# Gate projection with its two halves of the weights side by side

## The reference

```
px = (rmsnorm(x, norm1_g[l]) * (1.0 + sc1) + sh1) @ w_in[l] + b_in[l]
g = p[..., GATE_OFF:SGU_OFF]          # 16 columns
gates = (g[0], log_sigmoid(g[1]), g[2], log_sigmoid(g[3]))
b = cumsum(log_forget)                # per chunk of 128 tokens
```

## Time and profile before

| what | value |
|---|---|
| median of 3 runs | 2589.0 us |
| the profiled execution's own time | 2588.8 us |
| its span, first to last instruction | 2586.0 us |
| TensorE busy | 2521.5 us (98%) |
| VectorE busy | 1395.6 us (54%) |
| ScalarE busy | 777.0 us (30%) |
| GpSimd busy | 1548.5 us (60%) |
| granted TensorE clock, mean | 0.997 |

### The profile page before, as it was taken

One profiled execution on the slowest core, in us unless ns is written; L12 is line 12 of the kernel. 1 busy time (PEld: TensorE's weight loads), 2 busy tenths in 40 slices (PEclk: granted clock), 3 DMA queues, 4 the chain that ended last, 5 costly groups with the idle time before them and its releaser, 6 DMA issues.

```text
span 2586.0 us, 39643 instructions
## 1 busy us (share of the span) xinstructions
PE 2521.5 (98%) x14594; PEld 2083.6 (81%) x14594; DVE 1395.6 (54%) x2065; ACT 777.0 (30%) x1620; POOL 1548.5 (60%) x1625
## 2 busy tenths in 40 slices
PE   6999999999999999999999999999999999999999
PEld 5888988888888886888788887778888887777876
DVE  5864556742853758726433333444544555557854
ACT  3224353111111123245321212222222222443544
POOL 2433244765766665543777777776666676546563
PEclk9999999999999999999999999999999999999999
DMA  7341142332332322111223332433333333223231
GB/s 272 109 156 46 34 179 83 130 130 65 123 130 97 120 64 71 59 58 50 82 90 97 91 96 86 130 103 106 92 96 98 90 107 90 98 73 98 83 105 65
DMA packets 79264, 255.57 MB, mean 99 GB/s; under 512 B 9872, under 2 KB 13712, under 8 KB 78864
## 3 DMA queue, kind: packets, MB, share of 16 engines
q1 hardware_dynamic: 63136, 213.21, 25.4%
q10 hardware_dynamic: 15984, 40.40, 5.1%
HBM read 236.28 MB, written 2.10 MB: 92 GB/s over the span
## 4 chain that ended last, share of the span: by engine, by line
PE 88%; DVE 4%; issue 3%; POOL 2%; ACT 2%; DMA 1%; SPq 0%; ACTq 0%; POOLq 0%; DVEq 0%
PE PS L463 21%; PE PS L466 21%; PE PS L464 21%; PE PS L1664 4%; PE PS L1666 4%; PE PS L1665 4%; PE PS L725 1%; POOL w_lo L444 1%; PE PS L714 1%; PE PS L708 1%; PE PS L1520 1%; POOL w_hi L442 1%; DMA raw<-in_wout 1%; DVE Z L2415 1%; DVE XL L2422 1%
## 5 line engine op out<-in xcount | busy, mean ns | idle before, releaser
L444 POOL TENSOR_TENSOR w_lo<-raw,w_hi 128x512 fp32r<-128x512 f32 (+1 forms) x606 | 877.5, 1448 | 50.6
L463 PE MATMUL PS<-XH,w_hi 128*128 128x512 f32 (+1 forms) x2080 | 781.4, 376 | 16.9 <-DVE XL L2422 3.3
L464 PE MATMUL PS<-XL,w_hi 128*128 128x512 f32 (+1 forms) x2080 | 753.6, 371 | 0.0
L466 PE MATMUL PS<-XH,w_lo 128*128 128x512 f32 (+1 forms) x2080 | 705.9, 372 | 0.0
L437 POOL TENSOR_TENSOR word<-ones 128x1 f32<-128x1 f32 x303 | 96.6, 319 | 865.4 <-PE PS L466 539.5
L463 PEld LDWEIGHTS PS<-XH,w_hi 128*128 128x128 f32 x2080 | 391.3, 188 | 118.3 <-issue 9.3
L442 POOL TENSOR_SCALAR w_hi<-raw 128x512 fp32r<-128x512 f32 (+1 forms) x606 | 486.5, 803 | 0.0
L464 PEld LDWEIGHTS PS<-XL,w_hi 128*128 128x128 f32 x2080 | 391.5, 188 | 69.8
L466 PEld LDWEIGHTS PS<-XH,w_lo 128*128 128x128 f32 x2080 | 361.4, 188 | 55.0
L1664 PE MATMUL PS<-XH,w_hi 128*128 128x512 f32 (+1 forms) x640 | 230.8, 361 | 8.1 <-DVE XL L2422 8.1
L1666 PE MATMUL PS<-XH,w_lo 128*128 128x512 f32 (+1 forms) x640 | 224.9, 351 | 0.0
(11 more groups left out here) (346 smaller groups left out, 3522.1 us busy)
## 6 DMA issues: line engine op xcount, KB each, us to landing
raw<-in_wgu SPq DMA_DIRECT2D x88, 512.0 KB, 3.5
raw<-in_wa SPq DMA_DIRECT2D x80, 512.0 KB, 3.5
modt<-in_wmod SPq DMA_DIRECT2D x48, 512.0 KB, 10.1
raw<-in_win SPq DMA_DIRECT2D x48, 512.0 KB, 3.5
modv<-in_wmod ACTq DMA_DIRECT2D x48, 512.0 KB, 4.9
raw<-in_wdn SPq DMA_DIRECT2D x32, 512.0 KB, 3.5
QS<-Z ACTq DMA_DIRECT2D x96, 128.0 KB, 2.5
raw<-in_wout SPq DMA_DIRECT2D x16, 512.0 KB, 3.5
```

Source lines behind the costliest of these rows:

```text
L444: pool.tensor_tensor(lo, src, hi.bitcast(FP32), ALU.subtract).then_inc(s_split, 1)
L463: pe.matmul(acc(s)[:, a:b], hi, rh[:, i, a:b], start=i == 0, stop=False)
L464: pe.matmul(acc(s)[:, a:b], hi, rl[:, i, a:b], start=False, stop=False)
L466: last = pe.matmul(acc(s)[:, a:b], lo, rh[:, i, a:b], start=False, stop=i == k - 1)
```

## The change

The two halves of the gate weights are placed side by side as 32 columns of one tile `wgs`. One product of these 32 columns by `XH` and one by `XL` give 32 rows, of which rows 0 to 15 are of the upper weights and rows 16 to 31 of the lower ones. The product of the lower weights by `XL`, left out before, is now part of the result. The 32 rows are copied to `grow`. The six transposes become six products with a 32 by 16 matrix `gsum` of two identities one above the other, which turns the rows and adds the two groups at once. `gsum` is made once by GpSimd at the start.

```diff
-        wgh = place("wgh", [P, KT, 16], FP32R)
-        wgl = place("wgl", [P, KT, 16], FP32R)
+        wgs = place("wgs", [P, KT, 32], FP32R)
+        gsum = place("gsum", [32, 16])
...
-        grow = place("grow", [16, T], addr=addr_of["Z"] + 3 * T * 4)
+        grow = place("grow", [32, T], addr=addr_of["Z"] + 3 * T * 4)
...
+            pool.tensor_tensor(gsum[:], ident[0:32, 0:16], ident[0:32, 16:32], ALU.add).then_inc(s_gsum, 1)
...
-                        out = banks(4, 6)[0:16, a:b]
-                        pe.matmul(out, wgh[:, k, :], XH[:, k, a:b], start=k == 0, stop=False)
-                        pe.matmul(out, wgh[:, k, :], XL[:, k, a:b], start=False, stop=False)
-                        last = pe.matmul(out, wgl[:, k, :], XH[:, k, a:b], start=False, stop=k == KT - 1)
+                        out = banks(4, 6)[0:32, a:b]
+                        pe.matmul(out, wgs[:, k, :], XH[:, k, a:b], start=k == 0, stop=False)
+                        last = pe.matmul(out, wgs[:, k, :], XL[:, k, a:b], start=False, stop=k == KT - 1)
...
+                pe.wait_ge(s_gsum, 1)
                 for j in range(NJ):
-                    last = pe.transpose(PS[:, 7, 16 * j:16 * j + 16], grow[:, j * P:(j + 1) * P], ident[0:16, 0:16])
+                    last = pe.matmul(PS[:, 7, 16 * j:16 * j + 16], grow[:, j * P:(j + 1) * P], gsum[:], start=True, stop=True)
...
-                act.activation(wgh[:], wg[:], ACT.Copy).then_inc(s_wgh, 1)
+                act.activation(wgs[:, :, 0:16], wg[:], ACT.Copy).then_inc(s_wgh, 1)
...
-                act.activation(grow[:], banks(4, 6)[0:16, 0:T], ACT.Copy).then_inc(s_growe, 1)
+                act.activation(grow[:], banks(4, 6)[0:32, 0:T], ACT.Copy).then_inc(s_growe, 1)
...
-                dve.tensor_tensor(wgl[:], wg[:], wgh[:].bitcast(FP32), ALU.subtract).then_inc(s_wgl, 1)
+                dve.tensor_tensor(wgs[:, :, 16:32], wg[:], wgs[:, :, 0:16].bitcast(FP32), ALU.subtract).then_inc(s_wgl, 1)
```

More of the change, by code:

```diff
@@ L287, in build_program @@
         cz = place("cz", [P, KT, 32], addr=addr_of["YC"] + 16 * D)
-        cz2 = place("cz2", [P, KT, 32], addr=addr_of["wgh"])
+        cz2 = place("cz2", [P, KT, 32], addr=addr_of["wgs"])
         modt = {m: place(f"modt{m}", [P, KT, P], addr=a) for m, a in
@@ L384, in build_program @@
         s_grow = sem("gate_rows_done")
+        s_gsum = sem("gate_row_selector_made")
         s_growe = sem("gate_rows_evacuated")
```

## The result

The changed kernel takes 2595.2 us in the median of 14 runs, the kernel before 2590.05 us in 14 runs beside it. The ratio is 1.0021 (95% interval 1.0015 to 1.0028): slower by about 5 us. The forecast was a gain of 2.45 us, its range ended at 2590.6. The profiled execution has a span of 2592.7 us, 6.7 more than before. Two slow executions among all that follow, 5617.3 us (the kernel before, beside e1 to e4) and 2775.5 us (e2, at a granted clock of 0.85), are left out of the ratios and intervals, and the second of the median of e2.

What follows compares the result with a forecast made beforehand. TensorE was taken to bound the kernel (busy 2521.5 of 2586.0 us). Gains at forget_sums of 1.5 us in layer 0 and 0.95 in layer 1, together 2.45 off 2588.8, gave 2586.4 us; range 2583.5 to 2590.6.

Steps and rivals of the forecast that it cites:

- Gate products: TensorE, each layer: 16 of 48 gate products go, saving 2.78 us; the wider weight loads stay hidden and cost nothing.
- the cost without cover: Weight loads of the gate products, if not hidden under other products: 16 x 0.11 = 1.8 us; not counted.
- Selector: TensorE, replacing six transposes: 12 records at 0.09 us, 0.61 us more per layer (0.31 to 1.33); net saving 2.17.
- The small edits: Strided writes of wgs, copy of grow and GpSimd's making of gsum: claimed to add nothing.
- Layer 0's chain: VectorE's taps, then lf, delay forget_sums: start 78.2 instead of 79.70, gain 1.5 us (0.95 whole stall, 2.05 none).
- the stall: VectorE's two 24-element operations before lf, 1.33 us in layer 0; layer 0's chain taken at 1.3, between 0.75 and 1.86.
- the second rival: VectorE's taps, slowed beside GpSimd, hold forget_sums beyond today's start: 1.95 us slower in all, 2590.8 us; chance 0.13.
- Layer 1's chain: Three taps add 1.14 us, chain to lf takes 1.5 (0.9 to 2.07): forget_sums at 1019.75, gain 0.95 us (0.45 to 1.55).
- At the full clock: TensorE behind the gate projections, 64.78 to 200 and 1006 to 1100 us: read as running at 2.4 GHz.
- Time taken out of TensorE's stream reaches the end: TensorE, busy 2521.5 of 2586.0 us: savings shorten the whole unless a wait hidden today comes into sight.

Runs made afterwards that it cites:

- e1: The kernel before with 64 empty bytes where the changed kernel has its selector gsum, no instruction different: 2594.4 us, ratio 1.0019 to the kernel before.
- e4: The changed kernel with fewer VectorE convolution taps ahead of the gates (layer 0: 10, layer 1: 8, instead of 12): 2590.8 us, ratio 1.0005 to the kernel before.
- e2: The changed kernel with the selector gsum placed behind everything else, all other tiles at their earlier addresses: 2590.8 us, ratio 1.0009 to the kernel before.
- e3: The changed kernel run once more, unaltered, for a second trace: 2596.0 us, ratio 1.0025 to the kernel before.
- e7: The changed kernel with gsum placed behind everything else and fewer taps ahead of the gates (e2 and e4 together): 2586.2 us, ratio 0.9989 to the kernel before.
- e9: The kernel before with gcol moved ahead of XH and vrow behind XL, so XH and XL start at remainder 192 to 256 bytes: 2571.3 us, ratio 0.9932.
- e11: The kernel before with 192 empty bytes ahead of everything, all distances between tiles kept: 2590.9 us, ratio 1.0005 to the kernel before.
- e13: The kernel before with word and eps_c placed ahead of the weights, moving weights and four tiles behind them by 64 bytes, others staying: 2572.8 us, ratio 0.9934.
- e6: The kernel before with 128 empty bytes where e1 had 64: 2594.0 us, ratio 1.0019 to the kernel before.
- e12: The kernel before with 192 empty bytes where e1 had 64: 2592.9 us, ratio 1.0015 to the kernel before.

## Why the prediction was wrong, step by step

- *Gate products:* 2.78 us a layer forecast, 2.73 and 2.72 measured. Right, the free wider load too. (32 loads stay in a layer, not the 16 that the cost without cover counts; that cost entered no sum.)
- *Selector:* 12 records, right; 0.119 us each and not 0.09, between the bounds. The weight loads of 32 by 128 take 0.181 to 0.187 us in the trace, longer than the 0.133 to 0.138 of the transposes. Net 1.77 instead of 2.17 us a layer.
- *The small edits, "I count nothing":* the step that failed. I costed what `gsum` makes GpSimd do and not where it lies. Its 64 bytes move `HH` and `HL` against the weights; 1584 products lose 0.8 to 3.8 ns each (3.5 us), and e1 and e2, which put the same 64 bytes in and take them out, measure 5.1 us and 4 to 5 us. That alone turns the forecast around. No rival had it.
- *Layer 0's chain:* right in its mechanism, with luck in the taps and the stall nearly whole. The five taps were forecast to end at 76.85 and ended at 76.61. But the forecast's 1.10 a tap is the mean of four taps in the earlier trace rows, the first of which began before GpSimd's long operations and took 0.71, the others 0.96, 1.65 and 0.97. So the reading under the second rival, that less than a whole operation is added to each tap, holds of the mean and not of the single taps: a tap that begins during a GpSimd operation ends about 0.5 us after it. Here three taps did (0.96, 1.66, 0.97) and two did not, where the forecast had four at 1.10. The chain behind took 1.77 us and not 1.3. The gates began 0.25 us earlier in this trace, so the sums gained 1.0 us and not 1.5, the forecast's lower bound (0.95).
- *Layer 1's chain:* right in its mechanism, short in its size. The taps ended 1.18 us later (forecast 1.14, again with a mean of hindered and free taps), but the chain behind them took 3.11 and not 1.5 us, over my upper bound of 2.07: the moved chain met the stall at L2626 and again at L2630. `lf` was 1.6 us later than forecast, and that is the second rival's case in this layer: the sums started 0.7 us later than before against the stage's start (1024.16 - 2.76 = 1021.40, before 1020.69), under its 1.05.
- *"At the full clock":* I read it as given. Half the clock behind the wait in layer 1 cost 1.7 us in the first trace of the changed kernel. In e2 and e3 the same wait (2.35 and 2.28 us) was followed by the full clock. Stretches at half clock stand at 834 to 847, 979 to 994 and 1141 to 1151 us in some traces with the change and without it, so that the wait brought this one on is not shown.
- *"Time taken out of TensorE's stream reaches the end":* true once both costs are gone (e7: 2.7 us faster; TensorE's own saving is 3.5).

The gain of the products, the late taps and the place of `gsum` are each worth about 5 us or less of 2589, so a forecast of 2.45 us could not survive one of them overlooked.

## What to carry to other kernels

A new tile costs its place: in a kernel that is bound by TensorE, put it behind all others, or compare the distances of untouched products in the two traces before looking for a cause in the changed ones. When work is taken away ahead of a wait, the other engine's program order has to move with it; here the taps ahead of the gates, and with them the gain. And look for the cheap gain beside the question: 64 bytes between weights and moving operand, to 256, gave 17.5 us (e9), six times the 2.7 that the change could (e7).

## What the runs showed of the hardware

- TensorE's pace depends on the addresses of its two operands relative to each other: at 2.4 GHz 512-column fp32r products, each with a weight load of its own, stand 226.9 to 233.3 ns apart by the distance between weights and moving operand, to 256 bytes. The Trainium skill (SBUF — State Buffer, "Who interferes with whom") gives TensorE two independent read ports, one for moving data and one for weights, and says that it never waits on anyone. The runs differ on the two ports' independence: with all tiles moved together the pace stays (e11), with the moving operand alone (e9) or the weights alone (e13) it changes, over all distances by up to 3%, also where no other engine and no DMA is at work. e13 moved four other tiles with the weights, none of which these products read; that the weights are the partner rests on this and on those stretches. Why 0 bytes is worst in layer 0 and best in layer 1 is open; in layer 0 products of 512 and of 256 columns alternate.
- The same kernel can run a long stretch at another pace: 233.3 ns for the 512-column products from some 440 to 790 us in layer 0's feed-forward part in the first trace of the changed kernel and in e4, 231.5 in its second trace. e6 and e12 show it in parts of that stretch. What sets it is not shown.
- VectorE's small operations beside GpSimd can take five times as long (two copies of 24 elements 1.33 us in layer 1, 0.26 in layer 0). A long tap that begins during a GpSimd operation ends about 0.5 us after that operation's end: 0.96 or 1.66 us instead of 0.71 to 0.73, by the length of the operation (1.04 or 1.59).
